# Three of eight residual additions per half moved from VectorE to Pool in a two-block network

## The reference, cut to what matters

```
def rmsnorm(x, g):
    y = xf * lax.rsqrt(jnp.mean(xf * xf, axis=-1, keepdims=True) + NORM_EPS)
def modulated_norm(h, g, m, k):
    return rmsnorm(h, g) * (1.0 + m[..., k + 1, :]) + m[..., k, :]
def gated_residual(h, y, g, m, k, weight):
    return h + weight * m[..., k + 2, :] * rmsnorm(y, g)
...
h = half_ffn(h, ...)                                 # sub 0 (h and context)
h = gated_residual(h, y, ...)                        # sub 1 (differential attention)
h = half_ffn(h, ...)                                 # sub 2
...                                                  # second layer: sub 3, 4, 5 the same way
x = second_block(x, ...)
```

## Time and profile before

| | |
|---|---|
| median of three runs | 2516.59 us (2514.46 to 2521.89) |
| the profiled execution | 2515.36 us, its span 2513.6 us |
| PE busy | 2437.2 us (97%) |
| DVE busy | 1584.0 us (63%) |
| ACT busy | 1069.3 us (43%) |
| POOL busy | 0.2 us, 4 instructions |

### The profile page before, as it was taken

How to read it: one execution, slowest core, us unless ns; L and a number is a source line. 1 busy time by engine, 2 the same in 40 slices (tenths; PEclk the granted TensorE clock), 3 DMA queues, 4 the chain that set the end, 5 groups by cost and what they waited for, 6 DMA issues and landing times.

```text
span 2513.6 us, 36409 instructions
## 1 busy us (share of the span) xinstructions
PE 2437.2 (97%) x14732; PEld 2097.3 (83%) x14732; DVE 1584.0 (63%) x2825; ACT 1069.3 (43%) x1877; POOL 0.2 (0%) x4
## 2 busy tenths in 40 slices
PE   8999999999899999999999999899899999999998
PEld 4888888866688888888888887899898988999987
DVE  7767766366577766387523376555665867656756
ACT  4222325355552223252223366544545565455563
POOL 0000000000000000000000000000000000000000
PEclk9999999999999999999999999999999999999999
DMA  6555441211125445225422221355343523444432
GB/s 276 194 195 201 192 177 54 99 51 41 51 98 201 189 182 199 86 99 196 173 101 93 92 84 51 141 188 193 131 182 121 174 112 135 160 144 158 146 107 85
DMA packets 48697, 348.77 MB, mean 139 GB/s; under 512 B 5393, under 2 KB 5521, under 8 KB 6801
## 3 DMA queue, kind: packets, MB, share of 16 engines
q1 hardware_dynamic: 48530, 346.44, 37.2%
HBM read 345.36 MB, written 1.05 MB: 138 GB/s over the span
## 4 chain that ended last, share of the span: by engine, by line
PE 92%; DVE 5%; ACT 2%; issue 1%; DMA 0%; DVEq 0%; SPq 0%; ACTq 0%
PE ps L464 25%; PE ps L466 25%; PE ps L465 25%; DVE w_lo L1964 1%; PE ps L793 1%; PE ps L794 1%; PE ps L795 1%; PE ps L983 1%; ACT w_hi L1349 1%; PE ps L840 1%; PE ps L627 1%; PE ps L670 1%; PE ps L1009 1%; PE ps L827 1%; PE ps L652 1%
## 5 line engine op out<-in xcount | busy, mean ns | idle before, releaser
L1349 ACT ACTIVATE w_hi<-ring 128x1024 fp32r<-128x1024 f32 x504 | 533.7, 1060 | 1142.0 <-PE ps L466 1066.5
L1964 DVE TENSOR_TENSOR w_lo<-ring,w_hi 128x1024 fp32r<-128x1024 f32 x504 | 615.4, 1223 | 529.0 <-ACT w_hi L1349 526.7
L464 PE MATMUL ps<-u_hi,w_hi 128*128 128x512 f32 (+1 forms) x1856 | 660.0, 356 | 15.7 <-DVE u_lo L1979 8.4
L466 PE MATMUL ps<-u_hi,w_lo 128*128 128x512 f32 (+1 forms) x1856 | 650.9, 351 | 0.0
L465 PE MATMUL ps<-u_lo,w_hi 128*128 128x512 f32 (+1 forms) x1856 | 647.5, 349 | 0.0
L464 PEld LDWEIGHTS ps<-u_hi,w_hi 128*128 128x128 f32 x1856 | 349.3, 188 | 68.7 <-issue 17.0
L465 PEld LDWEIGHTS ps<-u_lo,w_hi 128*128 128x128 f32 x1856 | 349.7, 188 | 49.7 <-issue 0.5
L466 PEld LDWEIGHTS ps<-u_hi,w_lo 128*128 128x128 f32 x1856 | 349.3, 188 | 46.4
L464 PE MATMUL ps<-uh,w_hi 128*128 128x256 f32 x1184 | 341.7, 289 | 8.1 <-DVE ul L2402 5.6
L1952 DVE CUSTOM_DVE_ANT_0 waste<-ring,condb,cols 128x1024 f32<-128x1024 f32 x272 | 336.8, 1278 | 8.7 <-ACT condb L1597 7.7
L465 PE MATMUL ps<-ul,w_hi 128*128 128x256 f32 x1184 | 331.0, 280 | 0.0
(11 more groups left out here) (333 smaller groups left out, 2673.7 us busy)
## 6 DMA issues: line engine op xcount, KB each, us to landing
ring<-in_wk SPq DMA_DIRECT2D x324, 1024.0 KB, 4.8
hT<-in_x SPq DMA_DIRECT2D x1, 2048.0 KB, 15.4
htabs<-in_htabs SPq DMA_DIRECT2D x1, 1152.0 KB, 7.2
out_t<-uT SPq DMA_DIRECT2D x2, 512.0 KB, 2.7
trig<-in_trig SPq DMA_DIRECT2D x3, 256.0 KB, 7.1
wuk<-in_uk SPq DMA_DIRECT2D x2, 256.0 KB, 5.1
wuv<-in_uv SPq DMA_DIRECT2D x2, 256.0 KB, 4.9
cols<-in_cols SPq DMA_DIRECT2D x1, 302.5 KB, 3.0
```

What stands on the lines that cost most here:

```text
L464: mm(bank, hi, x_hi, start=first, stop=False, skip_group_check=skip)
L466: return mm(bank, lo, x_hi, start=False, stop=last, skip_group_check=skip)
L1349: f(half_hi(K, 0, HALF), ringed(n, K % 2 * HALF, (K % 2 + 1) * HALF), ACT.Copy).then_inc(whi_ready, 1)
L1964: tt(half_lo(K, 0, HALF), ringed(HALF_SLOT[K], K % 2 * HALF, (K % 2 + 1) * HALF), half_hi(K, 0, HALF).bitcast(F32), ALU.subtract).then_inc ...
```

## The change

Of the eight additions of a half, chunks 1, 3 and 5 (`H_POOL`) are made by Pool, chunks 0, 2, 4, 6 and 7 (`H_VECTOR`) by VectorE as before. VectorE makes all eight multiplications. Pool has a program of its own, 30 additions in ten halves, each waiting for its multiplication (yr_ready), and at B6 also for the addition whose chunk it overwrites. Pool's additions raise a new semaphore, hp_ready. ScalarE's squares wait in the old order, each for its own maker; SP waits for both semaphores; at B6 VectorE's additions 2, 6 and 7 wait for Pool's.

```diff
+H_POOL = (1, 3, 5)
+H_VECTOR = (0, 2, 4, 6, 7)
+NHV = len(H_VECTOR)
...
-                    sp.wait_ge(h_ready, 10 * KC)
+                    sp.wait_ge(h_ready, 10 * NHV)
+                    sp.wait_ge(hp_ready, 10 * len(H_POOL))
...
+            def h_chunk(part, c):
+                if c in H_POOL:
+                    act.wait_ge(hp_ready, part * len(H_POOL) + H_POOL.index(c) + 1)
+                else:
+                    act.wait_ge(h_ready, part * NHV + H_VECTOR.index(c) + 1)
...
-                    if ready is not None:
-                        act.wait_ge(ready, seen + (c + 1) * step_of)
+                    if part is not None:
+                        h_chunk(part, c)
...
-                    act.wait_ge(h_ready, h_seen + s * KC + c + 1)
+                    h_chunk(h_parts + s, c)
...
-                    if c:
+                    if c and c - 1 not in H_POOL:
                         n = (c - 1) * TT + s * S
                         dve.wait_ge(yr_ready, yrs - (c < KC))
                         tt(hT[:, n:n + S], hT[:, n:n + S], yT[:, n:n + S], ALU.add).then_inc(h_ready, 1)
...
-                            dve.wait_ge(h_ready, 9 * KC + (c - 1) // 2 + 1)
+                            over = (c - 1) // 2
+                            if over in H_POOL:
+                                dve.wait_ge(hp_ready, 9 * len(H_POOL) + H_POOL.index(over) + 1)
+                            else:
+                                dve.wait_ge(h_ready, 9 * NHV + H_VECTOR.index(over) + 1)
...
+        @block.gpsimd
+        def _(pool):
+            yrs = 0
+            for sub in range(6):
+                for s in range(2 if sub + 1 in PARTED else 1):
+                    for c in H_POOL:
+                        n = c * TT + s * S
+                        to = c * S if sub == 5 else n
+                        pool.wait_ge(yr_ready, yrs + c + 1)
+                        if sub == 5 and c // 2 in H_VECTOR:
+                            pool.wait_ge(h_ready, 9 * NHV + H_VECTOR.index(c // 2) + 1)
+                        elif sub == 5 and c // 2 != c:
+                            pool.wait_ge(hp_ready, 9 * len(H_POOL) + H_POOL.index(c // 2) + 1)
+                        nc.gpsimd.tensor_tensor(hT[:, to:to + S], hT[:, n:n + S], yT[:, n:n + S],
+                                                ALU.add).then_inc(hp_ready, 1)
+                    yrs += KC
```

More of the change, by code:

```diff
@@ L304, in program @@
         h_ready = sem("h_ready")
+        hp_ready = sem("hp_ready")
         rot_done = sem("rot_done")
@@ L1329, in _ @@
             steps = norms = 0
-            t_seen = h_seen = hid = mid = units = ofree = o_n = y_seen = 0
+            t_seen = h_parts = hid = mid = units = ofree = o_n = y_seen = 0
             eps = col("eps")
@@ L1357, in used, with squares @@
                 high()
-            def squares(T, ready, seen, step_of, to=sq, src_stride=TT):
+            def h_chunk(part, c):
[3 more added lines that the diff above has]
+                    act.wait_ge(h_ready, part * NHV + H_VECTOR.index(c) + 1)
+            def squares(T, part, to=sq, src_stride=TT):
                 for c in range(KC):
-                    if ready is not None:
-                        act.wait_ge(ready, seen + (c + 1) * step_of)
+                    if part is not None:
+                        h_chunk(part, c)
                     f(to[:, c * src_stride:c * src_stride + T], hT[:, c * src_stride:c * src_stride + T],
@@ L1407, in next_input @@
             def next_input(sub):
-                nonlocal h_seen
+                nonlocal h_parts
                 root(0)
@@ L1420, in next_input @@
                     piece_high(sub, c, 1)
-                h_seen += 2 * KC
+                h_parts += 2
             def ffn_tail(sub):
@@ L1608, in _ @@
                 if sub not in PARTED:
-                    squares(T, h_ready if sub else None, h_seen - KC, 1)
+                    squares(T, h_parts - 1 if sub else None)
                 if sub == 0:
@@ L1725, in _ @@
                         used()
-                h_seen += KC
+                h_parts += 1
             for lay in range(DEPTH):
                 if lay == 0:
-                    squares(S, h_ready, h_seen - KC, 1, sq2, S)
+                    squares(S, h_parts - 1, sq2, S)
                 norm(S)
```

## The result

The changed kernel took 2523.53 us (median of 20 runs, 2516.83 to 2533.74), the kernel before 2518.82 us on the same chip (20 runs, 2514.46 to 2525.42): a ratio of 1.0019, 95% interval 1.0010 to 1.0027. The forecast was 2512.1. The time lies inside the stated range, near its upper end, but the change makes the kernel 4.7 us slower by the medians where 4.5 us were to be gained, and the forecast's own range ended at 2515.

A forecast was written before the change was run, and what follows sets the result against it. TensorE is busy for 97% of the span, but VectorE's row sets the end of context halves at B1 to B4: 4.0 us there plus 0.5 at B6, 2515.36 - 4.5 = 2510.9, as median 2512.1; range 2508 to 2525.

The forecast's parts named there:

- What bounds the kernel: VectorE's 16 instructions set the end of context halves at B1 to B4, 4.0 us to gain; own halves 0.
- what Pool costs VectorE: All halves: Pool running beside VectorE was taken not to slow it, nothing in the sum; forecast's chance 0.48.
- Pool's own price: Each of Pool's 30 additions of 128x256, hand-over included, was taken at 0.6 us, without loss.
- Turns: Rival: Pool's addition holds VectorE's two-input SBUF instructions; 2514.8 us at D = 0.416, 2523.7 at 0.83; chance 0.32.
- B5 and B6: Sums there go at the low clock's pace; gain taken as 0 at B5 and 0.5 us at B6.
- D: Length in us of Pool's addition in rival Turns, worked out at 0.416, 0.83 and 1.22, against 0.336 saved.
- Starved: Rival: VectorE's queued instructions go first, Pool waits for a gap behind L1964; +19.4 us, 2535; chance 0.07.
- Pool late: Rival: no contention, but over 1.4 us per addition with hand-over, so squares 5 to 7 late; 2515.4; chance 0.07.
- Nothing arrives: Rival: halves end sooner, but low clock elsewhere or ring loads give the time back; 2515.4, give or take 2; chance 0.06.
- the new wait at B6: VectorE's addition 2 waits for Pool's 1, 6 and 7 for 3; no stall at 0.6 us, 0.6 at 1.22.

The follow-up runs named there:

- the versions beside PSUM: Changed kernel with Pool adding only two pieces each in the context halves of B1, B3 and B4; ratios 0.9996 and 0.9994 against the kernel before.

## Why the prediction was wrong

**What bounds the kernel** was right. The context halves decide: of the 6.05 us that B2's lost, 5.5 are still there at the start of B3 (368.40 against 362.88), and the medians differ by 4.7. The own halves cost nothing although their rows grew by 0.62 us: VectorE's wait of 0.73 us for the root took it in, and uT moved by 0.01 to 0.04 us.

**The step that failed** is "what Pool costs VectorE". The sum took nothing for it and 0.48 as its chance, with no row for or against, and so counted 1.0 us of gain in each context half of B1 to B4. Measured, these halves changed by -0.33, +6.05, +0.16 and -0.32 us. The traces show that no moved addition beside two-input instructions is free: either VectorE is held, 0.54 us where it saves 0.336, or Pool starves. Pool's own price was right (0.6 taken, 0.58 to 0.62 measured from the end of the VectorE instruction ahead of it), and so was the gain on VectorE's side where nothing held it: B2's weight half started 4.37 us after the first multiplication, 4.4 was forecast. The gain was lost because the squares follow Pool, not VectorE.

**Turns** was the mechanism of the own halves, of B5 and B6 and in part of the context halves of B1 and B4. Measured, its D is 0.54, between the two values that were worked out. It said that a two-input row loses, that rows with multiplications from PSUM still gain some 0.6 at D of 0.416 and lose 0.1 at 0.83 (measured -0.33 and -0.32 at B1 and B4), and that the own halves lose up to 0.25 (measured 0.01 to 0.04). It took two of three additions to lie beside such multiplications in B3 as well; there it is one of three. And its sum has a slip: two free additions and one that loses 0.49 make a gain of 0.2 at 0.83, not a loss of 0.1, so that the terms give some +7.5 instead of +8.3, and some +16 instead of +19 at 1.22. The Trainium skill, "SBUF — State Buffer", "Who interferes with whom", states this contention and that whoever issues first gets the shared ports for its whole instruction. The held multiplication, 0.95 us for 0.42, agrees. On who comes first the recorded starts don't fit it: in B2's context half Pool's addition was recorded from 717.06, 0.16 us behind the start of VectorE's addition as in B1's own half, and 11 instructions of VectorE that started later, the weight half among them, went ahead of it.

**Starved** was the mechanism of B2's context half and of one addition in B3's. Its working was nearly exact in size: the last square at 8.5 us forecast, 8.59 measured. Two things were missing. It was priced as all halves or none, with a point of decision ("more than one VectorE instruction on average") that doesn't exist; what goes with it in these runs is whether VectorE had paused shortly before. And it priced the late squares at 2.6 us, without the 3.4 us by which the sums then ended later, some 2.7 of them by the estimate above from the granted clock of 0.50 behind an idle time of 4.30 us, though the earlier trace rows showed such a stretch at B5 behind 2.75 us of idling. The term was mis-sized by more than half.

**Pool late** fell: where Pool got in, an addition is recorded with 0.72 to 0.91 us, under 1.4. **Nothing arrives** was right in one point: the 1.7 to 1.8 us that the versions beside PSUM won in their halves didn't show in the time; whether it was given back or drowned in the scatter isn't settled.

**B5 and B6**: forecast 0 and 0.5 gained, seen +0.27 and -0.30. Both times are inside what profiles without Pool there show (B5 7.93 to 8.91, B6 7.99 to 8.63), so neither is right or wrong by this. Whether the new wait at B6 would stall VectorE with 0.6 us per addition can't be read either, since each multiplication behind an addition of Pool is held anyway.

What stays open: why VectorE, once its row has run unbroken for some seven instructions, leaves no turn to Pool, while a gap of 35 ns does. The runs show when it happens, not the cause. That B2's context half is all of the loss is shown to the width of the intervals only: without it the ratio is 1.0012, and the interval reaches from 0.9993 to 1.0030.

## What to carry to other kernels

Work that is moved from VectorE to Pool should lie beside instructions of VectorE that read PSUM; beside instructions with two inputs in SBUF it cost VectorE more than it saved here (0.54 us against 0.336). Before moving a step on the critical path, look at the moved-to engine's turn in the longest unbroken row: there the late end is not one addition but the end of the row. And price a new wait of TensorE with the low clock behind it when the trace of before has such a stretch.

## What the runs showed of the hardware that I had not expected

Pool's additions of 128x256 are recorded with 0.72 to 0.91 us where they got in and with 1.18 to 5.33 us where they starved; where VectorE's instruction in the way had two inputs in SBUF, the end came 0.58 to 0.62 us after the end of that instruction. A recorded start of Pool is thus no sign that it works. The offset of that start to VectorE's addition, 0.16 us, was the same where Pool got in at once and where it starved; what differed was what VectorE had done just before, and a gap of 35 ns in VectorE's row was enough to let Pool in.
